# A two-layer decoder trunk on one core: the even mixer's queues woven together, I - X by VectorE and the inverse copied by ScalarE

## The chip, the cores and the metric

The kernel runs on one core of a Trainium2 chip. The metric is the device time of one execution in microseconds (us). TensorE multiplies matrices into PSUM, eight banks of 512 float32 columns; VectorE, ScalarE and GpSimd do elementwise work; SyncE issues the weight transfers. Each engine works through its own queue in order and waits on semaphores.

## The reference

512 tokens of width 1024 pass two layers. Each is: half a gated feed-forward product, a mixer, the other half product, and a gated embedding term; a norm ends it. The mixer of layer 0 (even) joins sliding-window attention and an RWKV-7 recurrence, that of layer 1 (odd) is a forgetting attention. What the change touches is the recurrence, 8 heads of 64:

```python
def step(state, inp):
    r_t, w_t, k_t, v_t, kk_t, a_t = inp
    s_kk = einsum('bhij,bhj->bhi', state, kk_t)
    state = state * w_t - s_kk * (kk_t * a_t) + v_t * k_t
    return state, einsum('bhij,bhj->bhi', state, r_t)
...
y = (y - mean) * rsqrt(var + GN_EPS) * ln_w + ln_b
y = y + sum(r * k * r_k) * v
out = concat([attention, y * g]) @ even_w_out
```

## The kernel before, in words

All float32 weights are used as a sum of two reduced parts: ScalarE writes `w_hi` (`split_hi`), VectorE `w_lo = w_raw - w_hi` (`split_lo`), and a tile of 128 columns costs three matmuls (`product`, L421). Weights come in jobs: SyncE loads a job's tiles into one of two slots, ScalarE and VectorE split it when the job two before is done, TensorE multiplies. In the even mixer's input projection a job has 16 tiles and fills two banks; in the output projections 8 tiles and one.

The even mixer runs in this order. `even_tensor` (L779) computes the projection in 160 groups of three matmuls, and between groups the attention of four head pairs; `even_scalar`, `even_vector` and `even_pool` hold the matching orders as strings (L920, L1048, L1097: J is a job's evictions and split, L logits, E exponentials, M a token-shift mix, S its difference on GpSimd). Then `rwkv_tensor`, `rwkv_scalar`, `rwkv_vector` and `rwkv_pool` (L1152 to L1619) treat the recurrence in chunks of 64 tokens, in two halves `h` of four heads, each as two pairs `q`, one half wholly behind the other (`rwkv_start`, L1147, waits for the half before). Within a half:
- the front: decays and scaled keys (`lora`, `sigmoids`, `lc`, `exps`, `kq`, `b_scaled`, `rq`, `k_scaled`, `rk_summed`, `bonus`) and their transposes (`turned`, L1200), which end in `ab` and `ak`, the products within chunks;
- the inverse of a triangular 64x64 block for each head and chunk, in levels 1 to 5. A level is X = A M (L1264), a mask on X by VectorE, M X' and X' M^T (L1270, L1272), and two subtractions by VectorE that renew `m_inv` and `mt_inv`;
- the output products `we`, `gq`, `h`, `yc`, and a chain of states over the chunks (`z`, L1301, and `state`, L1506), each step waiting for the other engine;
- the tail: `yz`, the gate `g`, the group norm (`y_raw` to `gn_normed`), `y_turned`, `y_weighted`, and the split into `y_hi` and `y_lo`.

The output projection's first two jobs are begun early (`out_begin`, L703), in the second half's tail. A step's semaphore counts all steps of its engine, so `due` (L1118) waits for one count of one engine. The table `RWKV_STEPS` (L73) is that order.

Of the kernel before, what the change touches and what calls it, by code (L numbers as in the profile page):

```python
# [62 lines left out]
def both(names):  # L63

    return [f"{name}:{q}" for name in names.split() for q in range(2)]


def each_pair(names):

    return [f"{name}:{q}" for q in range(2) for name in names.split()]  # L70


RWKV_STEPS = {  # L73
    "tensor": both("lora v_turned ss rk_summed kq_turned b_turned k_turned ab ak aab f")
    + [s for n in range(1, LEVELS - 1) for s in both(f"x{n}") + each_pair(f"mx{n} mxt{n}")]
    + both("x5 mxt5 we gq h yc") + [s for c in range(2, NC) for s in both(f"z{c}")]
    + both("yz g y_turned"),
    "scalar": both("""kk_squared sigmoids decay exps chunk_ends kq_by_token k_by_token f_copied we_copied
        h_copied yc_copied g_copied gn_squared gn_std"""),
    "vector": both("""lc lcm ka k rk v_summed v_by_token kk_clamped rn2 kq b_scaled rq k_scaled bonus  # L80
        b_by_token ab_masked ak_masked init m0""")
    + [s for n in range(1, LEVELS - 1) for s in both(f"x_masked{n}") + each_pair(f"m{n} mt{n}")]
    + both("x_masked5 mt5 gq_copied") + [s for c in range(1, NC) for s in both(f"state{c}")]
    + both("bonus_gated y_raw gn_summed gn_rinv gn_normed y_weighted y_done"),
    "pool": both("a_decayed masks_scaled b_tail k_tail diag mt_masked mt0"),
# [27 lines left out]
def trunk(nc, dram, out, stages=STAGES):  # L113

    ctx = ExitStack()
    with ctx:
# [10 lines left out]
        for st in stages:  # L127
# [104 lines left out]
        hb = view("hb", [P, 3 * RP, T + 1])  # L232
# [6 lines left out]
        swa_k = [view(f"swa_k{g}", [P, T]) for g in range(2)]  # L239
        swa_v = view("swa_v", [P, T])  # L240
        swa_vt = view("swa_vt", [P, NB, P])
        swa_logit = view("swa_logit", [P, 2, NB, 2 * P])
# [10 lines left out]

        constants_at = max(offset[0], int(behind_projections * 1024) + 16 * 1024 + 512)
        offset[0] = constants_at
# [4 lines left out]
        gn_eps = view("gn_eps", [P, 1])  # L260
        at(Y + 8)
# [3 lines left out]

        at(XN)
        kr = view("kr", [P, 2, 2, T])  # L270
        amb = view("amb", [P, 2, NC, 3, C])
        kf = view("kf", [P, 2, NC, 2, C])
        mt_inv = view("mt_inv", [P, 2, NC, C])
        at(W + 4)
        m_inv = view("m_inv", [P, 2, NC, C])
        at(W + 12)
        x1 = view("x1", [P, 2, NC, C])
        at(behind_projections)
        bk = view("bk", [P, 2, 2, T])
        ktok = view("ktok", [P, 2, NC, C])  # L280
        vtok = view("vtok", [P, 2, NC, C])
        chunk_end = view("chunk_end", [P, 2, NC])
        v_sum = view("v_sum", [P, 2, NC])
        rn2 = view("rn2", [P, 2, NC])
        gn_sum = view("gn_sum", [P, 2, NC])
        gn_dev = view("gn_dev", [P, 2, NC])
        gn_inv = view("gn_inv", [P, 2, NC])
        assert offset[0] <= constants_at
        at(Y + 12)
        bonus = view("bonus", [P, 2, T])  # L290
# [761 lines left out]
        def even_pool(pool, st):  # L1052
# [1206 lines left out]
```

## Time and profile before

| | before |
|---|---|
| median of 3 runs (lowest, highest) | 2234.67 us (2231.94, 2236.96) |
| profiled execution, its span | 2235.76 us, 2234.1 us |
| TensorE busy, matmuls | 2147.3 us (96%), 12522 |
| VectorE, ScalarE, GpSimd busy | 1126.0, 746.0, 347.8 us |
| mean granted clock of TensorE | 0.98 |
| even mixer, input projection to output projection | about 380 to 760 us of the span |
| odd mixer's output projection | from about 1764 us |

A row of the profile gives a source line, an engine, the operation as out<-in by the program's names, and durations. Matmul durations overlap, since matmuls are pipelined: the distance of starts tells the rate. A granted clock of 1.00 is 2.4 GHz, 0.50 is 1.2 GHz. "[5.64 <-...]" behind a row of the timeline is the engine's idle time ahead of it and what ended it.

### The profile page before, as it was taken

To read this page: it belongs to the slowest core of one execution; us is meant where nothing else is said; L and a number is where in the kernel's file an instruction comes from. 1 tells how busy PE (TensorE), PEld (TensorE's weight loads), DVE (VectorE), ACT (ScalarE), POOL (GpSimd) and SP (SyncE) were. 2 spreads that over 40 slices of the span, in tenths; PEclk is the share of its full clock that TensorE was granted. 3 is DMA by queue.
4 is the path that set the end of the run, shared out by engine and by line. 5 is a ranking of instruction groups with operands and counts; after the bars stand their busy time and mean duration, and the time that the engine had idled before them with its cause. 6 is when DMAs were issued, how large, how long until landed. Compare 5 with 4: busy or idle time off the path is not lost.

```text
span 2234.1 us, 32237 instructions
## 1 busy us (share of the span) xinstructions
PE 2147.3 (96%) x12522; PEld 1746.5 (78%) x12522; DVE 1126.0 (50%) x1337; ACT 746.0 (33%) x968; POOL 347.8 (16%) x352
## 2 busy tenths in 40 slices
PE   7999999996868999999999999999999899999998
PEld 6888888775857888888887888887667688888887
DVE  4443445556685644344565433445666454424464
ACT  4432223343122333122254422223444343312234
POOL 2000004444130300000330000013333320000032
PEclk9999999997979999999999999999999999999999
DMA  5323324320000433332333334324322143243232
GB/s 152 94 80 109 95 84 113 95 57 20 4 2 12 132 94 82 106 107 79 86 111 91 95 92 113 94 71 109 94 75 66 57 132 101 83 118 94 67 94 85
DMA packets 365116, 192.29 MB, mean 86 GB/s; under 512 B 9694, under 2 KB 362064, under 8 KB 365024
## 3 DMA queue, kind: packets, MB, share of 16 engines
q1 hardware_dynamic: 362784, 185.10, 30.0%
q0 software_dynamic: 2224, 5.86, 0.8%
q8 instruction: 70, 1.15, 0.2%
q14 instruction: 22, 0.18, 0.0%
q10 hardware_dynamic: 16, 0.00, 0.0%
HBM read 188.81 MB, written 2.13 MB: 85 GB/s over the span
## 4 chain that ended last, share of the span: by engine, by line
PE 92%; DVE 5%; ACT 2%; issue 1%; DMA 0%; POOL 0%; SPq 0%; ACTq 0%; POOLq 0%; DVEq 0%
PE bank L427 24%; PE bank L428 24%; PE bank L429 24%; PE bank L1182 3%; PE bank L1683 2%; PE bank L1685 2%; PE bank L1684 2%; PE bank L795 2%; PE bank L797 2%; PE bank L796 2%; PE bank L1700 1%; PE bank L1719 1%; PE bank L1730 1%; DVE w_lo L417 1%; ACT w_hi L412 1%
## 5 line engine op out<-in xcount | busy, mean ns | idle before, releaser
L427 PE MATMUL bank<-xn_hi,w_hi 128*128 128x512 f32 x1416 | 554.9, 392 | 10.9 <-DVE w_lo L2190 6.0
L428 PE MATMUL bank<-xn_hi,w_lo 128*128 128x512 f32 x1416 | 552.6, 390 | 0.0
L429 PE MATMUL bank<-xn_lo,w_hi 128*128 128x512 f32 x1416 | 552.4, 390 | 0.0
L412 ACT CAST w_hi<-w_raw 128x2048 fp32r<-128x2048 f32 (+3 forms) x211 | 336.3, 1594 | 624.0 <-PE bank L429 560.1
L417 DVE TENSOR_TENSOR w_lo<-w_raw,w_hi 128x2048 fp32r<-128x2048 f32 (+3 forms) x209 | 441.6, 2113 | 151.2 <-ACT w_hi L412 149.8
L427 PEld LDWEIGHTS bank<-xn_hi,w_hi 128*128 128x128 f32 x1416 | 266.9, 188 | 69.5 <-DVE w_lo L2190 6.3
L428 PEld LDWEIGHTS bank<-xn_hi,w_lo 128*128 128x128 f32 x1416 | 266.8, 188 | 56.1 <-issue 1.0
L429 PEld LDWEIGHTS bank<-xn_lo,w_hi 128*128 128x128 f32 x1416 | 266.8, 188 | 55.7
L429 PE MATMUL bank<-h_lo,w_hi 128*128 128x512 f32 x704 | 273.9, 389 | 0.0
L427 PE MATMUL bank<-h_hi,w_hi 128*128 128x512 f32 x704 | 273.9, 389 | 0.0
L428 PE MATMUL bank<-h_hi,w_lo 128*128 128x512 f32 x704 | 273.9, 389 | 0.0
L581 DVE TENSOR_TENSOR act_in<-bank,rinv 128x512 f32<-128x512 f32 x88 | 60.8, 691 | 368.5 <-PE bank L429 368.5
L463 POOL TENSOR_TENSOR sq_sum<-x 128x512 f32<-128x512 f32 x8 | 8.3, 1039 | 1325.5 <-DVE x L599 1236.3
L429 PEld LDWEIGHTS bank<-h_lo,w_hi 128*128 128x128 f32 x704 | 132.1, 188 | 27.6
L427 PEld LDWEIGHTS bank<-h_hi,w_hi 128*128 128x128 f32 x704 | 132.1, 188 | 27.4
L428 PEld LDWEIGHTS bank<-h_hi,w_lo 128*128 128x128 f32 x704 | 132.1, 188 | 27.4
L599 DVE SCALAR_TENSOR_TENSOR x<-bank,x 128x512 f32 (+1 forms) x64 | 44.2, 691 | 204.6 <-PE bank L429 204.6
L558 ACT CAST h_hi<-prod 128x512 f32 (+1 forms) x88 | 54.6, 621 | 181.7 <-DVE prod L588 181.7
L427 PE MATMUL bank<-y_hi,w_hi 128*128 128x512 f32 x256 | 102.1, 399 | 7.4 <-DVE w_lo L417 6.0
L429 PE MATMUL bank<-y_lo,w_hi 128*128 128x512 f32 x256 | 100.5, 393 | 0.0
L428 PE MATMUL bank<-y_hi,w_lo 128*128 128x512 f32 x256 | 100.2, 392 | 0.0
L591 DVE TENSOR_TENSOR h_lo<-prod,h_hi 128x512 f32 (+1 forms) x88 | 60.9, 692 | 76.3 <-ACT h_hi L558 76.3
(345 smaller groups left out, 2624.3 us busy)
## 6 DMA issues: line engine op xcount, KB each, us to landing
w_raw<-in_ffn_w_gu_dram SPq DMA_DIRECT2D x176, 512.0 KB, 5.0
w_raw<-in_ffn_w_down_dram SPq DMA_DIRECT2D x64, 384.0 KB, 3.9
w_raw<-in_ffn_w_down_dram SPq DMA_DIRECT2D x64, 320.0 KB, 3.7
w_raw<-in_even_w_in_dram SPq DMA_DIRECT2D x20, 512.0 KB, 4.5
w_raw<-in_ple_w_gate_dram SPq DMA_DIRECT2D x16, 512.0 KB, 3.8
w_raw<-in_fox_w_in_dram SPq DMA_DIRECT2D x16, 512.0 KB, 5.2
w_raw<-in_even_w_out_dram SPq DMA_DIRECT2D x16, 256.0 KB, 3.2
w_raw<-in_fox_w_in_dram SPq DMA_DIRECT2D x16, 256.0 KB, 4.3
```

The costliest lines, as they stand in the source:

```text
L412: nc.scalar.copy(w_hi[slot][:, 0:tiles], w_raw[slot][:, 0:tiles]).then_inc(w_hi_ready, 1)
L417: nc.vector.tensor_tensor(w_lo[slot][:, 0:tiles], w_raw[slot][:, 0:tiles], w_hi[slot][:, 0:tiles].bitcast(F32), ALU.subtract).then_inc(w_r ...
L427: nc.tensor.matmul(dst, w[0], hi[:, k], start=k == 0, stop=False)
L428: nc.tensor.matmul(dst, w[1], hi[:, k], start=False, stop=False)
L429: last = nc.tensor.matmul(dst, w[0], lo[:, k], start=False, stop=k == tiles - 1)
L558: nc.scalar.copy(h_hi[:, ds(j)], prod[:]).then_inc(h_hi_ready, 1)
L581: nc.vector.tensor_tensor(act_in[:], bank[2 * slot][:], rinv[:], ALU.mult).then_inc(act_in_ready, 1)
L591: nc.vector.tensor_tensor(h_lo[:, ds(j)], prod[:], h_hi[:, ds(j)].bitcast(F32), ALU.subtract).then_inc(h_ready, 1)
L795: nc.tensor.matmul(dst, hi, xn_hi[:, k], start=k == 0, stop=False)
L796: nc.tensor.matmul(dst, lo, xn_hi[:, k], start=False, stop=False)
L797: mm = nc.tensor.matmul(dst, hi, xn_lo[:, k], start=False, stop=k == DT - 1)
L1182: mm = nc.tensor.matmul(dst[of_chunk(c), at:at + width], lhsT(j, of_chunk(c)), rhs(j, of_chunk(c)), start=k == 0, stop=k == len(operands) - 1)
```

## The change

1. The even input projection has 20 jobs of 8 tiles and one bank instead of 10 of 16, and the query columns come ahead of the low-rank ones; the recurrence's columns come by halves of heads (keys, receptances, values of the first half first).
2. The recurrence's front is cut into functions, 8 on TensorE, 8 on ScalarE, 11 on VectorE and 4 on GpSimd. The first half's stand between projection jobs (F in the strings), the second half's between the first half's levels. The first half's tail stands between the second half's levels. Tiles of the two halves lie apart, and each group of steps has a semaphore of its own (`RWKV_SEMAPHORES`, `seen`).
3. The levels: GpSimd masks A beforehand (`a_level`), VectorE makes I - X from PSUM (`one_less_x`), TensorE forms the whole new inverse and its transpose, and ScalarE copies both from PSUM (`level_done`). Before, VectorE masked X and subtracted twice.
4. Between the steps of the second half's chain of states stand groups of the output projection.
5. Both mixers' output projections use the lower and the upper half of the weight buffers in turn, so that a job is split two jobs ahead.

```diff
-                jobs.phase(st + "in", [2 * DT] * (2 + 2 * RP))
+                jobs.phase(st + "in", [DT] * (4 + 4 * RP))
...
-        FIRST_WINDOW, APART = 18, 24
+        FIRST_WINDOW, APART = 27, 22
...
+            between += [(g, part, ()) for g, part in zip((118, 122, 127, 131, 139, 145, 152, 158), front)]
...
-            for what in "J0 E0 J1 J2 C0 E1 H0 J3 C1 E2 J4 H1 J5 C2 E3 H2 J6 C3 J7 H3".split():
+            for what in ("J0 J1 T0 J2 J3 J4 E0 J5 J6 C0 J7 E1 T1 H0 J8 J9 C1 E2 J10 H1 J11 F0 J12 C2 E3 J13 H2 F1 F2 "
+                         "J14 F3 J15 F4 C3 F5 J16 H3 F6 J17 J18 F7 J19").split():
...
+            for what in ("J0 J1 J2 L0 J3 J4 D0 J5 L1 J6 J7 T1 D1 V0 J8 L2 J9 M0 J10 M1 V1 D2 L3 J11 M2 J12 M3 V2 "
+                         "J13 M4 D3 M5 F0 J14 F1 F2 J15 F3 M6 F4 V3 J16 F5 M7 F6 F7 F8 J17 M8 F9 J18 M9 F10 "
+                         "J19 M10 M11").split():
...
+            for what in "N0 N1 S0 S1 S2 N2 S3 S4 S5 N3 S6 F0 S7 F1 S8 F2 F3 S9 S10 S11".split():
...
-                    for q in range(2):
-                        due(dve, f"x{level}", h, q)
-                        tt(x1[:, q], by_chunk(rb(q, 2)[:]), mask(MASK_L + level), ALU.mult, f"x_masked{level}")
...
-                            tt(m_inv[:, q], m_inv[:, q], by_chunk(rb(q, 3)[:]), ALU.subtract, f"m{level}")
...
-                        tt(mt_inv[:, q], mt_inv[:, q], by_chunk(rb(q, 0)[:]), ALU.subtract, f"mt{level}")
+            def one_less_x(h, level):
+                for q in range(2):
+                    level_seen(dve, "x", h, level, q)
+                    if level > 1:
+                        level_seen(dve, "mxt", h, level - 1, q)
+                    nc.vector.tensor_tensor(m_x[:, q, 1], over_chunks(eye[:]), by_chunk(rb(q, 2)[:]), ALU.subtract
+                                            ).then_inc(R["x_copied"], 1)
...
+            def level_done(h, level):
...
+                        nc.scalar.copy(m_x[:, q, 0], by_chunk(rb(q, 3)[:])).then_inc(R["m"], 1)
...
+                    nc.scalar.copy(mt_inv[:, q], by_chunk(rb(q, 0)[:])).then_inc(R["mt"], 1)
...
+            def a_level(h, level):
...
+                    nc.gpsimd.tensor_tensor(a_lev[:, q], am0[h][:, q], over_chunks(masks[:, MASK_LT + level]),
+                                            ALU.mult).then_inc(R["a_level"], 1)
...
+        def upper(j):
+
+            return j // 2 % 2
...
+            for n, j, slot, ahead in out_jobs(st):
+                if j + 2 < DT:
+                    out_split_hi(act, st, j + 2)
+                    gain_hi(act, norms[st] + 1, j)
```

TensorE's queue behind the first half's `ab` and `ak`, up to level 2. Before (`x` is the masked X):

```order
L1171 MATMUL bank<-kr,bk 64x128 x64
L1182 MATMUL bank<-eye,amb 64x64 x32
L1182 MATMUL bank<-vtok,akm 64x64 x32
L1182 MATMUL bank<-m_inv,amb 64x64 x32
L1182 MATMUL bank<-x,mt_inv 64x64 x16
L1182 MATMUL bank<-mt_inv,x 64x64 x16
L1182 MATMUL bank<-x,mt_inv 64x64 x16
L1182 MATMUL bank<-mt_inv,x 64x64 x16
L1182 MATMUL bank<-m_inv,amb 64x64 x32
```

Now (`m_x` holds the inverse and I - X; L1212 is `lora_w`, L1219 `lora_a`, L1198 `v_turned`, all of the second half):

```order
L1456 MATMUL bank<-kr,bk 64x128 x64
L1469 MATMUL bank<-eye,am_0 64x64 x32
L1469 MATMUL bank<-vtok,akm 64x64 x32
L1212 MATMUL bank<-th,lora_wa 128x512 x2
L1469 MATMUL bank<-m_x,a_lev 64x64 x32
L1219 MATMUL bank<-th,lora_wa 128x512 x2
L1469 MATMUL bank<-m_x,mt_inv 64x64 x16
L1469 MATMUL bank<-mt_inv,m_x 64x64 x16
L1469 MATMUL bank<-m_x,mt_inv 64x64 x16
L1469 MATMUL bank<-mt_inv,m_x 64x64 x16
L1198 MATMUL bank<-ident,hb 128x128 x8
L1469 MATMUL bank<-m_x,a_lev 64x64 x32
```

The second half's front moved into the first half's levels. VectorE's queue there, levels 1 to 3, now (L1841 is `one_less_x`, the rest the second half's front):

```order
L1841 TENSOR_TENSOR m_x<-eye,bank 128x512 x2
L1322 SCALAR_TENSOR_TENSOR act_in<-chunk_start,kr 128x512
L1322 SCALAR_TENSOR_TENSOR other<-chunk_start,kr 128x512
L1326 TENSOR_TENSOR kr<-act_in,kr 128x512
L1326 TENSOR_TENSOR kr<-other,kr 128x512
L1348 TENSOR_REDUCE v_sum<-bank 128x8 x2
L1352 SCALAR_TENSOR_TENSOR vtok<-v_sum,bank 128x512 x2
L1841 TENSOR_TENSOR m_x<-eye,bank 128x512 x2
L1332 TENSOR_SCALAR bk<-tmp,vecs 128x512 x2
L1336 SCALAR_TENSOR_TENSOR tmp<-bk,hb 128x512 x2
L1359 TENSOR_SCALAR rn_1<-bank 128x8 x2
L1363 RECIPROCAL rn_1<-rn_1 128x8 x2
```

Before, this queue had the masks and the subtractions of the levels and nothing else.

## Rows read from the trace of the kernel before

**Rows 1.** The page: busy time of each engine, share of the span, instructions.

```profile
PE 2147.3 (96%) x12522; PEld 1746.5 (78%) x12522; DVE 1126.0 (50%) x1337; ACT 746.0 (33%) x968; POOL 347.8 (16%) x352
```

**Rows 2.** Stretches of the span: length, busy of each engine, granted clock, DMA share, GB/s.

```profile
519.00:554.00 35.00, 16.34 (x75) 10.03 (x75) 30.12 (x37) 12.16 (x21) 16.36 (x10) 0.66 0.05 15
...
604.00:651.00 47.00, 23.31 (x184) 14.46 (x188) 35.72 (x60) 17.75 (x30) 12.96 (x8) 0.69 0.00 1
...
660.00:703.00 43.00, 40.69 (x1328) 39.35 (x1328) 25.51 (x49) 4.91 (x14) 2.63 (x2) 1.00 0.02 4
...
800.00:820.00 20.00, 20.00 (x90) 16.57 (x89) 9.74 (x10) 8.79 (x8) 0.00 (x0) 1.00 0.28 75
```

**Rows 3.** TensorE's waits, 522 to 722: us in total, times, longest.

```profile
PE bank L1229 <- DVE rn L1440: 17.5, 2, 9.0
```

**Rows 4.** Timeline of TensorE: start, length, line and operation, [idle before <-releaser].

```profile
525.19 1.19 PE L1215 MATMUL bank<-th,lora_wa 64*128 64x512 f32 x1 [5.64 <-issue]
...
544.01 1.04 PE L1202 MATMUL bank<-ident,kr 128*128 128x128 f32 x8
...
553.86 5.42 PE L1171 MATMUL bank<-kr,bk 64*64 64x128 f32 x128
...
563.72 1.15 PE L1182 MATMUL bank<-m_inv,amb 64*64 64x64 f32 x32 [0.70 <-DVE m_inv L1392]
...
590.96 3.60 PE L1182 MATMUL bank<-kf,mt_inv 64*64 64x128 f32 x62
...
603.51 0.40 PE L1301 MATMUL bank<-x,bk 64*64 64x64 f32 x8
...
659.88 1.15 PE L1182 MATMUL bank<-m_inv,amb 64*64 64x64 f32 x32 [0.70 <-DVE m_inv L1392]
...
704.20 1.98 PE L1311 MATMUL bank<-gate_in,lora_g 128*128 128x512 f32 x4
```

**Rows 5.** Timeline of VectorE in the first half's front.

```profile
533.46 0.68 DVE L1397 SCALAR_TENSOR_TENSOR sq<-bk,hb 128x512 f32<-128x512 f32 x1
...
534.66 1.77 DVE L1397 SCALAR_TENSOR_TENSOR bonus<-hb,vecs,sq 128x512 f32<-128x512 f32 x1
...
541.41 2.38 DVE L1397 SCALAR_TENSOR_TENSOR kr<-hb,vecs,tmp 128x512 f32<-128x512 f32 x1
```

**Rows 6.** Timeline of ScalarE in the first half's front.

```profile
526.53 1.28 ACT L1333 ACT_TABLE_LOAD   x1
...
544.64 1.08 ACT L1324 ACTIVATE kf<-bank 128x512 f32<-128x512 f32 x2 [8.94 <-PE bank L1202]
```

**Rows 7.** Timeline of GpSimd ahead of the first half's levels.

```profile
558.60 2.05 POOL L1588 TENSOR_TENSOR kr<-eye,chunk_end 128x512 f32<-128x512 f32 x2 [5.84 <-PE bank L1171]
560.60 2.50 POOL L1588 TENSOR_TENSOR mt_inv<-amb,masks 128x512 f32<-128x512 f32 x2
563.06 3.40 POOL L1588 TENSOR_TENSOR mt_inv<-eye,mt_inv 128x512 f32<-128x512 f32 x2
```

**Rows 8.** Timelines of VectorE and ScalarE at the projection's start and in a job.

```profile
389.02 3.35 DVE L487 RECIPROCAL rinv<-rms 128x512 f32<-128x512 f32 x1 [1.18 <-ACT rms L482]
393.86 2.80 DVE L937 TENSOR_TENSOR swa_k<-bank,rinv 64x512 f32<-64x512 f32 x4 [1.49 <-PE bank L797]
...
506.61 1.21 DVE L417 TENSOR_TENSOR w_lo<-w_raw,w_hi 128x1024 fp32r<-128x1024 f32 x1
...
505.40 1.06 ACT L412 CAST w_hi<-w_raw 128x1024 fp32r<-128x1024 f32 x1 [3.47 <-PE bank L797]
```

**Rows 9.** Timeline of TensorE at both mixers' output job 2.

```profile
722.98 0.49 PE L427 MATMUL bank<-y_hi,w_hi 128*128 128x512 f32 x1 [2.65 <-DVE w_lo L417]
...
1768.58 0.49 PE L427 MATMUL bank<-y_hi,w_hi 128*128 128x512 f32 x1 [3.34 <-DVE w_lo L417]
...
1769.56 0.63 PE L427 MATMUL bank<-y_hi,w_hi 128*128 128x512 f32 x1
```

**Rows 10.** DMA issues: line, count, KB each, median us to landing, 392 to 519.

```profile
w_raw<-in_even_w_out_dram SPq DMA_DIRECT2D x6, 256.0 KB, 3.1
```

More of the change, by code:

```diff
@@ L59 @@
     """.split()
[L63 to L85, printed above, removed]
+RWKV_SEMAPHORES = {
+    "front_products": "lora_w lora_a v_turned ss rk_summed kq_turned b_turned k_turned",
+    "front_activations": "kk_squared sig_w sig_a decay exps chunk_ends kq_by_token k_by_token",
+    "front_decays": "lc lcm", "front_values": "v_summed v_by_token", "front_norms": "kk_clamped rn2",
+    "front_elements": "ka k rk kq b_scaled k_scaled bonus rq b_by_token",
+    "front_tails": "a_decayed b_tail k_tail masks_scaled",
+    "pair_products": "ab ak aab f", "pair_masks": "ab_masked ak_masked init m0", "inverse_start": "mt_masked mt0 diag",
+    "f_copied": "f_copied", "a_level": "a_level", "x": "x", "x_copied": "x_copied", "mx": "mx", "mxt": "mxt",
+    "m": "m", "mt": "mt",
+    "chunk_products": "we gq h yc", "chunk_copies": "we_copied h_copied yc_copied", "gq_copied": "gq_copied",
+    "z": "z", "state": "state",
+    "tail_products": "yz g y_turned", "tail_activations": "gn_squared g_copied gn_std",
+    "tail_elements": "y_raw gn_summed bonus_gated gn_rinv gn_normed y_weighted y_done",
 }
@@ new lines, in rwkv_tensor @@
+            xs(1, 2)
+            yz(0, 1)
+            ms(1, 2)
+            xs(1, 3)
+            g(0)
+            ms(1, 3)
+            xs(1, 4)
+            ms(1, 4)
+            y_turned(0)
+            xs(1, 5)
+            ms(1, 5)
+            w_and_e(1)
+            gq(1)
+            hs(1)
+            yc(1)
+            for c in range(1, NC - 1):
+                z(1, c)
+                if c > 1:
+                    out_begin(pe, st, 0, c - 2, c - 1)
+            out_begin(pe, st, 0, NC - 3, OUT_BEGUN["even"])
@@ new lines, in rwkv_vector @@
+            front[5]()
+            one_less_x(0, 4)
+            front[6]()
+            front[7]()
+            front[8]()
+            one_less_x(0, 5)
+            front[9]()
+            front[10]()
+            gq_copied(0)
+            states(0)
+            ab_masked(1)
+            ak_masked(1)
+            start_inverse(1)
+            one_less_x(1, 1)
+            y_raw(0, 0)
+            one_less_x(1, 2)
+            y_raw(0, 1)
+            gn_summed(0)
+            one_less_x(1, 3)
@@ L1610, in rwkv_pool @@
[L1610 to L1619 removed]
+                    seen(pool, "ab", h, q)
@@ L1625, in unit_cols @@
+            front = rwkv_front_pool(pool, st, 1)
+            start_inverse(0)
+            a_level(0, 1)
+            diag(0)
+            a_level(0, 2)
+            front[0]()
+            a_level(0, 3)
+            a_level(0, 4)
+            front[1]()
+            a_level(0, 5)
+            front[2]()
+            front[3]()
+            start_inverse(1)
+            a_level(1, 1)
+            diag(1)
+            for level in range(2, LEVELS):
+                a_level(1, level)
         def unit_cols(u):
```

1315 lines of the change are left out of this document (796 added, 519 removed).

## The prediction

> **What bounds the kernel now.** I read the page first: TensorE is busy for 2147.3 of 2234.1 us and VectorE for half of it [rows 1]. So a gain can only come from stretches in which TensorE idles or runs slowly. The table by stretches shows two, both in the even mixer [rows 2]: TensorE is busy 16.3 of 35 us from 519 to 554 and 23.3 of 47 us from 604 to 651, with a granted clock of 0.66 and 0.69; in the inverse levels (660 to 703) it is busy 40.7 of 43 us at full clock. The waits name what ends the idle time: 17.5 us in two waits of `rk_summed` (L1229) for VectorE [rows 3]. The timeline [rows 4] tells the order: projection and attention end at 519.6 (the row at 525.19, less its idle 5.64), the first half's own products begin at 553.86, its levels at 563.72, its output products at 590.96, its chain of states at 603.51, and the second half's levels only at 659.88. The weights are not the bound: 256 KB land in 3.1 us [rows 10], one projection job's worth in two such transfers.
>
> **The change, part by part.** I compare the same marks before and after. All is worked out against the profiled execution (2235.8 us, span 2234.1), 1.1 above the median of the runs. "Front" is the elementwise and turning work ahead of `ab`, "half" a set of four heads.
>
> (a) *The first half's front moves under the projection.* TensorE still has to do it: six products 512 wide (1.98 for two, so about 5.7), 32 transposes (8 in 1.04, less at full clock, about 3.5) and `ss` (16 narrow ones, set at 0.8): 10 us [rows 4]. Now it is between projection groups. New waits, from the orders of the queues:
> - Jobs of 8 tiles halve the time in which a bank must be emptied and the next weights split. At the start VectorE ends the reciprocal at 392.4, then needs 2.8 for `swa_k`, which empties job 0's bank, and 1.2 for job 2's `w_lo`: 396.4 [rows 8]. TensorE is through with jobs 0 and 1 (the 16 groups that were one job) at 393.8, where `swa_k` began. Cost 2.6.
> - `v_by_token` stands on VectorE behind the split of job 15, and `ss` waits for it: 2.6. `kq_turned` waits for `bonus`, fourth in a block of five pieces: 1.9. The last bank must be emptied before `ab`: 0.8.
> The other jobs I take as covered: 24 matmuls at 20 us for 90 [rows 2] are 5.4 us, ScalarE's half split is 1.06 and VectorE's 1.21 [rows 8], a pass over a bank 0.68 [rows 5], so 2.4 us are left in each job for what stands ahead in the queue. `ab` begins at 519.6 + 10 + 7.9 = 537.5 instead of 553.9: **gain 16.4**.
>
> (b) *From `ab` to the first level.* Before: 9.9 us. Now VectorE has two tiles left to mix, and GpSimd must make `mt_masked`, `mt0` and the masked copy `a_lev` before the first product; the first two took 2.50 and 3.40 for the two pairs of heads, the cheapest op there half of 2.05 [rows 7]. 1.3 for `ab`, 3 for the mixing and `ab_masked`, 5.9 and 1.2 on GpSimd and the hand-overs give 12.1: **loss 2.2**.
>
> (c) *The first half's levels, with the second half's front inside.* The levels alone took 27.2. The inverse is now copied by ScalarE (half of 1.08 a copy [rows 6]) and I - X made by VectorE (one pass of 0.6 where three stood), both shorter than TensorE's 16 products (27.2 us for 28 such sets, 0.97): the split of the work as such is worth nothing, because the levels were TensorE-bound. It frees VectorE 2.4 us a level, in which the front fits. TensorE gets 8.1 more (10 less the `lora_w` products that fall into b). Waits: `sig_a` is behind the whole first level on ScalarE, and `v_turned` behind it, 1.9; `a_lev` and `bonus` about 1.1. Then VectorE and GpSimd slow each other: the same form of VectorE op takes 0.68 alone and 1.77 and 2.38 while GpSimd works [rows 5, 7]. With 16 such ops in the stretch the bounds are 0 and 16 times 1.4, 22 us. I take 6, nearer the low end, as TensorE has work queued between most of them. 27.2 + 8.1 + 3 + 6 = 44.3: **loss 17.1**.
>
> The Trainium skill (SBUF — State Buffer, on the engine ports) says that VectorE ops with two SBUF inputs and GpSimd ops that read SBUF take one shared port pair in turn, each for its whole length. By that rule VectorE can be held no longer than GpSimd works: 16 ops of this stretch at half of 2.05, 16.4 us instead of my bound of 22, and the sum would be 2207 at worst; the trace agrees in kind, 1.77 for 0.68 beside an op of GpSimd.
>
> (d) *Output products* of each half: as before, 0.4 for a wait on `k_by_token`: **loss 0.4**.
>
> (e) *Between the halves.* From the first chain of states (603.51) to the second half's first level (659.88) there were 56.4 us of tail, front and `ab`. Now the front is done and the tail comes later. What is left: six steps of the chain, with the two `ab` of the other half between them, 6.3; then `ab_masked` (VectorE, four passes of half width, 1.4 a pair of heads by the 0.68 of a whole one), `mt_masked`, `mt0` and `a_lev` on GpSimd, 8.5, with 4 us of TensorE work within. 14.8: **gain 41.6**.
>
> (f) *The second half's levels, with the first half's tail inside.* 27.2 + 4.2 for `yz`, the gate (1.98) and `y_turned`; the fourth I - X stands behind `gn_normed` on VectorE, which waits for a square root behind level 3 and a table load (1.28, [rows 6]) on ScalarE: 4: 35.4, **loss 8.2**. The chain of states takes 5.9 instead of 3.9, since output-projection groups stand between its steps: **loss 2.0** (they come back in g).
>
> (g) *The tail of the second half.* Before, from the last state (703.1, just ahead of the gate product's 704.20) to output job 2 at 722.98: 19.9 us, 2.65 of them for its `w_lo` [rows 9]. Now `y_raw` doesn't wait for the gate, no table load stands in it, 4 us of output groups are done, and job 2's weights go to the buffers' upper halves and are split before job 0's result is wanted. 13.3: **gain 6.6**.
>
> (h) *The odd mixer's output projection* gets the same early split: 3.34 of waiting goes, and the slow matmuls behind it (start to start 0.43 instead of 0.23, some eight of them): **gain 5.0** [rows 9].
>
> Sum: 16.4 - 2.2 - 17.1 - 0.4 + 41.6 - 8.2 - 2.0 + 6.6 + 5.0 = 39.7. 2235.8 - 39.7 = **2196 us**.
>
> **The rivals.**
> - *VectorE and GpSimd as the bound of the first levels.* If the slowing costs 14 instead of 6, and 4 more under the projection, where the first half's front meets the evictions and splits: 2208. For it: 1.77 and 2.38 in rows 5. Against: before, TensorE idled there, so every delay showed. Chance 0.25.
> - *The stalls don't come.* The waits of (a), (c) and (f) are worked; of the 7.9, 9 and 4 us, two thirds may not come if the queues interleave better than I see, 14 less: 2182. Chance 0.18.
> - *The small projection jobs starve TensorE (slower).* Each of some 18 jobs has 2.4 us to spare, and the attention's exponentials and logits (E and L in the strings) stand whole between the splits. If every job came 3 us late, 54 us would be lost, 2196 + 54 = 2250; it decides the sign from 2.2 us a job. Against: VectorE was busy 50% of the whole [rows 1], and there are four such blocks for 20 jobs. Chance 0.04.
> - *The overlap fails because a shared bank or buffer puts the front back in line:* about half of (e) lost, 2217. Chance 0.04.
>
> **How the numbers follow.** The forecast, 2196 with 2188 to 2204, gets 0.49. The range takes in both neighbouring rivals but not their far ends: 2179 to 2213. Faster by over 0.2% (about what a measurement of this kernel can tell from no change, 4.5 us): all but the starving case and a remnant, 0.95; within it 0.01; slower 0.04.
>
> **What would show it.** `ab` of the first half at about 537, the levels 44 us long at full clock instead of 27, the second half's levels some 15 us behind the first chain of states, no wait for `w_lo` ahead of output job 2 in either mixer, and the granted clock near 1 all through. It is wrong if TensorE waits for `w_lo` in the projection again and again, if the first half's levels take over 52 us, or if idle time above 10 us is left between the halves.

## The result, and the profile after

The changed kernel takes 2217.2 us (median of 4 runs, 2216.4 to 2217.8), the kernel before 2234.2 (2231.9 to 2237.0): ratio 0.9923, 95% interval 0.9906 to 0.9940. It is faster, as forecast, but by 17 us where 39.7 were worked out, and 2217.2 lies above the range (2179 to 2213). The profiled execution took 2217.2 (span 2215.6), 18.5 less in span than before.

The page of the changed kernel, busy time of each engine:

```profile
PE 2151.0 (97%) x12778; PEld 1749.5 (79%) x12778; DVE 1106.0 (50%) x1319; ACT 766.2 (35%) x1013; POOL 374.3 (17%) x376
```

Its stretches of the even mixer: from:to, length, busy time (number) of TensorE, its weight load, VectorE, ScalarE and GpSimd, granted clock, DMA share, GB/s.

```profile
392.40:519.60 127.20, 117.81 (x633) 90.48 (x632) 80.04 (x115) 58.23 (x130) 51.65 (x63) 0.97 0.23 67
519.60:548.75 29.15, 23.20 (x101) 17.64 (x99) 19.88 (x23) 6.48 (x9) 16.00 (x11) 0.89 0.12 36
560.40:605.00 44.60, 39.76 (x954) 35.17 (x954) 30.91 (x41) 19.43 (x35) 24.22 (x17) 0.96 0.01 3
605.00:632.40 27.40, 22.43 (x816) 21.05 (x816) 14.07 (x36) 6.39 (x17) 10.76 (x10) 1.00 0.02 4
632.40:671.70 39.30, 34.01 (x972) 32.15 (x972) 15.63 (x25) 13.76 (x24) 14.08 (x11) 0.91 0.01 4
```

The two dead stretches of [rows 2] are gone: from 605 to 632.4, between the halves, TensorE is busy 22.4 of 27.4 us. But the projection, 2.3 us from full before, is not: from 392.4 to `ab` TensorE idles 15.3 of 156.35 us. The timeline of TensorE shows where, and the marks that answer to [rows 4], the moments at which a part begins: start, length, operation, [idle before <-releaser].

```profile
395.67 0.80 PE L831 MATMUL bank<-xn_hi,w_hi 128*128 128x512 f32 x1 [2.77 <-DVE w_lo L410]
...
508.46 1.54 PE L874 MATMUL bank<-ident,swa_p 128*128 128x128 f32 x6 [3.49 <-ACT swa_pt L950]
...
528.70 1.23 PE L1198 MATMUL bank<-ident,kr 128*128 128x128 f32 x8 [1.40 <-DVE bonus L1391]
...
543.46 1.94 PE L1198 MATMUL bank<-ident,tmp 128*128 128x128 f32 x8 [3.77 <-DVE btok L1398]
545.05 0.78 PE L831 MATMUL bank<-xn_hi,w_hi 128*128 128x512 f32 x1
545.62 0.63 PE L832 MATMUL bank<-xn_hi,w_lo 128*128 128x512 f32 x1
...
548.75 0.49 PE L1456 MATMUL bank<-kr,bk 64*64 64x128 f32 x4 [0.79 <-DVE hb L995]
...
560.41 1.15 PE L1469 MATMUL bank<-m_x,a_lev 64*64 64x64 f32 x32
...
595.80 1.23 PE L1198 MATMUL bank<-ident,kr 128*128 128x128 f32 x8 [1.90 <-DVE act_out L1391]
...
604.98 3.89 PE L1469 MATMUL bank<-kf,mt_inv 64*64 64x64 f32 x126 [0.33 <-ACT ktok L1313]
...
619.01 0.22 PE L1587 MATMUL bank<-am,bk 64*64 64x64 f32 x1
...
632.43 1.15 PE L1469 MATMUL bank<-m_x,a_lev 64*64 64x64 f32 x32 [1.96 <-POOL a_lev L2031]
...
661.33 1.58 PE L1469 MATMUL bank<-m_x,mt_inv 64*64 64x64 f32 x32 [4.74 <-DVE m_x L1841]
...
671.72 3.89 PE L1469 MATMUL bank<-kf,mt_inv 64*64 64x64 f32 x126
...
686.27 0.40 PE L1587 MATMUL bank<-am,bk 64*64 64x64 f32 x8
...
693.95 1.16 PE L1456 MATMUL bank<-am,bk 64*64 64x64 f32 x64
...
705.05 0.50 PE L420 MATMUL bank<-y_hi,w_hi 128*128 128x512 f32 x1 [3.04 <-DVE y_lo L1909]
...
709.35 0.53 PE L420 MATMUL bank<-y_hi,w_hi 128*128 128x512 f32 x1
```

`kr` turned is `kq_turned`, the two `tmp` are `b_turned` and `k_turned`. 548.75 is `ab`, 560.41 and 632.43 the first level of each half, 604.98 and 671.72 their output products, 619.01 and 686.27 their chains of states, 709.35 the output projection's job 2, which now waits for no `w_lo`. Why `k_turned` was late stands in the timeline of VectorE:

```profile
537.81 1.46 DVE L410 TENSOR_TENSOR w_lo<-w_raw,w_hi 128x1024 fp32r<-128x1024 f32 x1
541.20 1.51 DVE L1076 SCALAR_TENSOR_TENSOR hb<-act_out,vecs,hb 128x512 f32<-128x512 f32 x1 [1.94 <-POOL act_out L1130]
542.64 1.27 DVE L1398 TENSOR_TENSOR btok<-bank,rn 128x512 f32<-128x512 f32 x2
```

and in that of GpSimd:

```profile
533.80 6.37 POOL L1435 TENSOR_TENSOR am<-masks,rn 128x512 f32<-128x512 f32 x4
540.13 1.03 POOL L1130 TENSOR_TENSOR act_out<-hb 128x512 f32<-128x512 f32 x1
```

VectorE stood from 539.3 to 541.2 in front of a tile to mix, whose shift GpSimd made only behind its four scaled masks; `b_by_token`, for which TensorE waited, was the next piece in VectorE's queue; what it reads had been ready since 535.6, when TensorE ended `b_turned`. The 3.49 at 508.46 is of the same kind: ScalarE copied the first turned probabilities (507.35) behind the four exponentials `exps` (505.26 to 507.4).

The marks give each term of the sum its measured size:

| term | forecast | measured | from |
|---|---|---|---|
| (a) `ab`, first half | +16.4 | +5.1 | 553.86 to 548.75 |
| (b) to the first level | -2.2 | -1.8 | 9.86 to 11.66 |
| (c) first half's levels | -17.1 | -17.3 | 27.24 to 44.57 |
| (d) output products, first half | -0.4 | -1.5 | 12.55 to 14.03 |
| (e) between the halves | +41.6 | +43.0 | 56.37 to 13.42 |
| (f) second half's levels | -8.2 | -12.1 | 27.2 to 39.29 |
| its output products | 0 | -2.5 | 12.05 to 14.55 |
| its chain of states | -2.0 | -3.7 | 3.94 to 7.68 |
| (g) last state to output job 2 | +6.6 | +4.5 | 19.87 to 15.40 |
| (h) odd mixer's output projection | +5.0 | +4.4 | lead 14.1 ahead of it, 18.5 at the end |
| sum | +39.7 | +18.1 | span: 18.5 |

The largest miss is (a), 11.3 of the 21 us. Of the rest, (f) is 3.9, the output products of both halves 3.6, the chain 1.7 and (g) 2.1. In (h), the lead is by how much the changed kernel is ahead at the odd mixer's first output product and at the end.

The marks count from the start of the span, and executions do not reach the mixer at the same moment: TensorE's first projection product starts at 381.80 before and at 380.96 now. Counted from there `ab` comes after 172.1 and 167.8 us, so that 0.8 of the 5.1 in (a) arose ahead of the mixer.

### The profile page after: what moved, and what is told of

It reads as the page before. It is cut to its first block, busy times and chain, and to the rows that moved or that the text cites. A ratio compares the mean times of both kernels' runs of the same rounds, so it can differ in the third digit from the quotient of the medians.

```text
span 2215.6 us, 32685 instructions
## 1 busy us (share of the span) xinstructions
PE 2151.0 (97%) x12778; PEld 1749.5 (79%) x12778; DVE 1106.0 (50%) x1319; ACT 766.2 (35%) x1013; POOL 374.3 (17%) x376
## 3 DMA queue, kind: packets, MB, share of 16 engines
HBM read 188.81 MB, written 2.13 MB: 86 GB/s over the span
## 4 chain that ended last, share of the span: by engine, by line
PE 91%; DVE 3%; ACT 2%; issue 2%; POOL 2%; DMA 0%; SPq 0%; POOLq 0%; DVEq 0%; ACTq 0%
PE bank L420 25%; PE bank L422 24%; PE bank L421 24%; PE bank L1469 3%; PE bank L2113 2%; PE bank L2115 2%; PE bank L2114 2%; PE bank L831 1%; PE bank L2130 1%; PE bank L833 1%; PE bank L832 1%; PE bank L2149 1%; PE bank L2160 1%; DVE w_lo L410 1%; ACT w_hi L405 0%
## 5 line engine op out<-in xcount | busy, mean ns | idle before, releaser
L405 ACT CAST w_hi<-w_raw 128x2048 fp32r<-128x2048 f32 (+3 forms) x209 | 325.7, 1559 | 637.8 <-PE bank L422 560.0
L410 DVE TENSOR_TENSOR w_lo<-w_raw,w_hi 128x2048 fp32r<-128x2048 f32 (+3 forms) x207 | 423.3, 2045 | 148.1 <-ACT w_hi L405 147.2
L420 PEld LDWEIGHTS bank<-h_hi,w_hi 128*128 128x128 f32 x704 | 132.2, 188 | 27.4
L592 DVE SCALAR_TENSOR_TENSOR x<-bank,x 128x512 f32 (+1 forms) x64 | 44.3, 692 | 205.6 <-PE bank L422 205.6
```

The costliest lines, as they stand in the source:

```text
L405: nc.scalar.copy(w_hi[slot][:, 0:tiles], w_raw[slot][:, 0:tiles]).then_inc(w_hi_ready, 1)
L410: nc.vector.tensor_tensor(w_lo[slot][:, 0:tiles], w_raw[slot][:, 0:tiles], w_hi[slot][:, 0:tiles].bitcast(F32), ALU.subtract).then_inc(w_r ...
L420: nc.tensor.matmul(dst, w[0], hi[:, k], start=k == 0, stop=False)
```

## The experiments

Theory Q: what is missing was lost to the order of the queues, an instruction that was ready behind one that was not. Theory E: the engines, slowed by each other, are at their limit, and a wait that is removed comes back elsewhere. The kernel before had medians of 2233.4 to 2234.0 beside these runs.

**The changed kernel again.**

> The changed kernel itself beside the others: 2217, within 1 us of its earlier runs. It measures how far the chips and runs of one kernel differ, under either theory.

Measured: 2217.8 (2215.7 to 2222.3). A difference of 1 us between medians says nothing here; marks in the traces say more. Counted from the first projection product, `ab` comes after 167.3 us here and 167.8 in the first trace. But the first half's levels take 46.1 here and 44.6 there, the same instructions at a granted clock of 0.93 and 0.96:

```profile
560.40:606.50 46.10, 41.25 (x954) 36.61 (x954) 30.90 (x41) 19.44 (x36) 24.26 (x17) 0.93 0.01 3
```

So half a us in the place of `ab` means something, 1.5 us in the length of these levels does not.

**ScalarE's copies of the probabilities first.**

```diff
-"J14 F3 J15 F4 C3 F5 J16 H3 F6 J17 J18 F7 J19"
+"J14 F3 K0 J15 K1 F4 F5 J16 H3 F6 J17 J18 F7 J19"
```

K0 and K1 are the two halves of C3, the copies of the fourth pair.

> ScalarE copies the turned probabilities of the fourth pair before the four exponentials of the decay, and its first two copies before the split of job 15's turn. Theory Q (the missing time under the projection is set by the order of the queues): the wait of 3.49 us ahead of the second set of probability transposes (508.46) goes, and with it the slow clock behind it, about 1 us; `ab` begins 4 us earlier, near 544.5, and the kernel takes 2213. Theory E (the engines, slowed by each other, are the limit): the exponentials are later by the two copies, `a_decayed` and what follows on VectorE are as late as before, the wait comes back at `kq_turned` or `k_turned`, and `ab` stays within 1 us of 548.75.

Measured: 2217.0 (2215.0 to 2218.8), no change. The wait went and another came 1.2 us behind its place (timeline of TensorE):

```profile
509.70 1.47 PE L1233 MATMUL bank<-head_ones,bk 128*128 128x2 f32 x12 [3.04 <-DVE vtok L1352]
```

This is the wait of `ss` for `v_by_token`, which the prediction had priced at 2.6 and the changed kernel did not show: both were there, one behind the other. `ab` came at 547.26, 1.5 earlier (1.1 counted from the first projection product). By this run alone theory E looks right.

**`b_by_token` ahead of the ninth tile.**

```diff
-"... J18 M9 F10 J19 M10 M11"
+"... J18 F10 M9 J19 M10 M11"
```

> VectorE makes `b_by_token` before it mixes the ninth tile, so it no longer stands behind a tile whose shift GpSimd makes only after its 6.4 us of scaled masks. Theory Q: the wait of 3.77 us ahead of `k_turned` (543.46) shrinks to under 1, and the granted clock of 0.50 from 545 to 550 rises; `ab` begins 5 us earlier (3 of wait, 2 of clock), 543.5, kernel 2212. Theory E: the mixing is still as late, the last job's split behind it too, and the gain is under 1.5 us.

Measured: 2210.8 (2209.1 to 2211.6), 7 us off for two pieces exchanged in VectorE's queue. The timeline of TensorE:

```profile
539.61 1.23 PE L1198 MATMUL bank<-ident,tmp 128*128 128x128 f32 x8 [0.33 <-DVE btok L1398]
543.01 1.21 PE L1456 MATMUL bank<-kr,bk 64*64 64x128 f32 x36 [0.78 <-DVE hb L995]
```

3.4 of wait is gone, and `ab` is 5.7 earlier (5.2 if one takes off that this execution had started the mixer 0.56 sooner). The levels behind it took 43.0 instead of 44.6, so that 1.6 of the 7 us may be their spread. Theory Q, and a term that the prediction had not under the projection: the clock.

**Matmuls that compute nothing.** Twelve of them in front of `k_turned`, added to the changed kernel.

```diff
+                if h == 0:
+                    for i in range(12):
+                        nc.tensor.matmul(bank[4][:], xn_hi[:, 0, 0:P], xn_hi[:, 0], start=True, stop=True)
```

> The changed kernel with twelve matmuls of 128x512 that compute nothing (into a free bank) put ahead of TensorE's turning of `k`, where it idled 3.77 us; at 0.23 each they fill 2.7 of them. They add work that the output does not use. If the granted clock of 0.62 from 540 to 550 comes from TensorE's own idle time ahead of it, it stays near 1, `ab` begins 1.5 to 2.5 us earlier than 548.75 and the kernel takes 2215 to 2216. If the clock falls for another reason, `ab` stays within 0.5 us.

Measured: 2213.9 (2211.9 to 2215.9), 3 to 4 us faster than without them; `ab` at 546.24. The timeline of TensorE, the filler and what follows it:

```profile
538.93 2.88 PE L1260 MATMUL bank<-xn_hi 128*128 128x512 f32 x12
542.85 1.23 PE L1198 MATMUL bank<-ident,tmp 128*128 128x128 f32 x8 [1.04 <-DVE btok L1401]
```

The stretch from 540 to 550 with the filler (columns as above):

```profile
540.00:550.00 10.00, 8.14 (x150) 6.49 (x149) 6.83 (x9) 3.46 (x5) 2.59 (x3) 1.00 0.01 2
```

The same stretch of the changed kernel without the filler:

```profile
540.00:550.00 10.00, 5.75 (x38) 4.68 (x42) 4.33 (x5) 3.18 (x5) 3.21 (x4) 0.62 0.00 1
```

The wait ended no sooner (542.85, in an execution that ran 0.55 ahead), but the granted clock stayed at 1 and the work behind it ran at full speed: 0.98 for the eight transposes instead of 1.59, 0.23 a matmul instead of 0.43. So an idle 3.8 us costs 3.8 and then 2 more. The rest of the 3 to 4 us is not in this trace, which is of the slowest of the four executions. The Trainium skill (TensorE: Matmul & The Clock Gate, on the HAM clock gate) says that a gate sets the clock by how busy TensorE has been of late; here the trace agrees.

**GpSimd's scaled masks ahead of its tails.** They got a semaphore of their own for it.

```diff
-"N0 N1 S0 S1 S2 N2 S3 S4 S5 N3 S6 F0 S7 F1 S8 F2 F3 S9 S10 S11"
+"N0 N1 S0 S1 S2 N2 S3 S4 S5 N3 S6 F0 S7 F3 F1 S8 F2 S9 S10 S11"
```

> The changed kernel with one edit on GpSimd: the four scaled masks (6.4 us, from 533.8) are made ahead of the tails of `b` and `k`, in the 15 us in which GpSimd idled before 526. What the wait of `k_turned` (3.77) rests on: under the order theory the ninth tile's shift comes some 4 us earlier, VectorE's two `rq` passes run alone (1.3 for both instead of 2.98), the wait shrinks to under 1, and the kernel takes 2211 to 2213, as with `b_by_token` moved. If the slowing of VectorE by GpSimd is what costs, it moves to the passes that now run beside the masks and the gain is under 3 us: 2215 or more.

Measured: 2210.1 (2207.2 to 2218.2). The wait of `k_turned` is 0.66, `ab` at 542.30, 5.2 earlier counted from the first projection product, as with `b_by_token` moved; the four masks took 4.05 instead of 6.37, in a stretch where VectorE idled, and the two `rq` passes 2.13 instead of 2.98 (1.3 was expected). The same wait goes from the other end of the chain, as theory Q says.

**The last pair's values and the elementwise work early,** on top of `b_by_token` moved.

```diff
-ScalarE: "... J16 H3 F6 ..."     VectorE: "... F4 V3 J16 F5 M7 F6 F7 F8 J17 ..."
+ScalarE: "... H3 J16 F6 ..."     VectorE: "... F4 F5 F6 F7 V3 J16 M7 F8 J17 ..."
```

> On top of `b_by_token` ahead of the ninth tile, ScalarE rounds the last pair's attention output before the split of job 16's turn, and VectorE scales `kq`, `b` and `k` ahead of the low part of that output, in the 6.7 us in which it idled before 521. Theory Q (queue order): the wait of 1.40 for `bonus` ahead of `kq_turned` goes, GpSimd's tails and scaled masks start up to 8 us earlier, no wait is left at `k_turned`; `ab` begins 1.5 to 2 us before its 543.0 of the run with `b_by_token` moved alone, and the kernel takes 2209 against 2210.8. Theory E (engine limit): the ops that were moved run beside GpSimd now and lose what they gain; 2210.8 stays.

Measured: 2210.7 (2207.9 to 2215.5). No wait is left at `kq_turned` or `k_turned` and `ab` comes at 541.37, 1.6 before the 543.01 and 2.4 counted from the first projection product; the medians can't show it. Worked by the trace, a small yes for theory Q.

**The fourth I - X of the second half first.**

```diff
             bonus_gated(0)
-            gn_normed(0)
             one_less_x(1, 4)
+            gn_normed(0)
```

> In the second half VectorE makes the fourth I - X before it normalises the first half's tail. Theory Q: the wait of 4.74 us at 661.33 goes and the slow clock behind it (1.5 us) too; a new wait of up to 1.5 us stands at the tail's transposes; the second half's levels take 34 to 36 us instead of 39.3 and the kernel 2212. Theory E: GpSimd's last level mask and VectorE's gate product (3.36 us for two) hold the level anyway, and the levels stay above 38.

Measured: 2214.8 (2213.8 to 2215.5), 3 us off instead of 6; the levels take 38.0, where the two traces of the changed kernel have 39.3 and 38.8, so the trace shows only about 1 of the 3. The wait shrank from 4.74 to 3.29 only, because `bonus_gated`, the gate product, still stood ahead (timeline of VectorE):

```profile
658.04 3.36 DVE L1876 SCALAR_TENSOR_TENSOR bonus<-bonus,vecs,tail_g 128x512 f32<-128x512 f32 x2 [5.16 <-ACT tail_g L1733]
661.32 1.27 DVE L1841 TENSOR_TENSOR m_x<-eye,bank 128x512 f32<-128x512 f32 x2
```

VectorE idled 5.16 for ScalarE's copy of the gate, and the two passes took 3.36 beside GpSimd's level mask, 1.40 for the same two in the second half's tail, where GpSimd rested.

**All orders at once.** The copies first; `v_by_token` ahead of `rk` and of the split (`F1 F3 J15 F2`); `b_by_token` and the elementwise work as above; the fourth I - X ahead of both `bonus_gated` and `gn_normed`.

> All the moves together: ScalarE's copies of the fourth pair's probabilities ahead of the exponentials, `v_by_token` on VectorE ahead of the split of job 15's turn (it took the place of that wait when the copies alone were moved: 3.04 us), `b_by_token` ahead of the ninth tile, the early elementwise work, and in the second half's levels the fourth I - X ahead of both the gate product and the normalisation. Theory Q: waits of 3.5, 3.8 and 1.4 under the projection and of 4.7 in the levels are gone, each with its slow clock; `ab` begins at 538 to 540 (the predicted 537.5), the second half's levels take 34 to 35, and the kernel takes 2202 to 2205. Theory E: the waits come back elsewhere, 2208 or more.

Measured: 2199.6 (2196.2 to 2203.4), 18 us less than the changed kernel and 2.4 below what was expected; ratio to before 0.9845 (0.9827 to 0.9864). TensorE's waits from 392 to 549: us in total, times, longest.

```profile
PE bank L831 <- DVE w_lo L410: 3.3, 2, 2.8
PE bank L857 <- DVE swa_logit L1029: 2.4, 2, 1.7
PE bank L1469 <- DVE am L1807: 1.3, 2, 1.1
PE bank L1456 <- DVE hb L995: 0.8, 1, 0.8
PE bank L1198 <- DVE bonus L1391: 0.6, 1, 0.6
```

The stretches of the same run: projection, first and second half's levels.

```profile
392.40:536.80 144.40, 137.17 (x732) 105.19 (x732) 100.96 (x137) 64.65 (x138) 68.70 (x74) 0.99 0.23 66
548.40:594.50 46.10, 41.28 (x952) 36.63 (x952) 30.90 (x41) 19.36 (x36) 24.28 (x17) 0.93 0.01 3
622.00:655.00 33.00, 32.47 (x972) 30.52 (x972) 14.54 (x25) 13.60 (x24) 13.58 (x11) 0.95 0.02 4
```

`ab` begins at 536.8, 156.4 us behind the first projection product where it was 167.8, and the second half's levels take 33.0 with nothing for TensorE to wait for. The engines had room for this front; the order did not use it. Theory E falls here. The copies moved alone had gained nothing only because the next instruction in line was late too.

**The value tile first,** on top of that.

```diff
-            firsts = [SWA_Q, SWA_Q + P] + ...
+            firsts = [SWA_Q + P, SWA_Q] + ...
```

> On top of all the moved orders, the projection turns out the attention's value tile first and its key tile second, so that the first bank is emptied by one pass of VectorE behind the reciprocal instead of four (0.7 instead of 2.8). If the first wait (2.77 us at 395.7) is set by that emptying and the split behind it, it shrinks to 0.5 to 1 and the second job's four passes are hidden behind job 2's 5.4 us of matmuls: 2 us earlier, 2197.5. If job 3 then waits for the same passes, nothing is gained: 2199.6.

Measured: 2196.2 (2195.5 to 2201.2), ratio to before 0.9836 (0.9813 to 0.9859): the fastest that was found, with the next one. The projection's first wait is 0.79 instead of 2.77, one of 0.15 came at 412, and `ab` begins at 532.4, 3.5 earlier counted from the first projection product, where 2 were expected: the wait that went is 2.0, and the slow clock behind it 1.5. The stretch from 390 to 400 of the changed kernel:

```profile
390.00:400.00 10.00, 7.23 (x25) 5.57 (x24) 7.43 (x8) 1.04 (x1) 8.61 (x22) 0.83 0.36 107
```

and of this run:

```profile
390.00:400.00 10.00, 9.21 (x43) 7.29 (x42) 6.98 (x10) 2.69 (x3) 8.62 (x21) 1.00 0.38 107
```

**The turned tiles behind the levels' products,** on top of the value tile first.

```diff
-            front[2]()
             xs(0, 2)
+            front[2]()
             ms(0, 2)
```

and `kq_turned` behind `xs(0, 5)`, `b_turned` behind `ms(0, 5)`, VectorE's `one_less_x(0, 2)` ahead of `front[3]`.

> On top of the kernel with the value tile first, in the first half's levels TensorE turns `v` behind the second level's first product and `kq` behind the fifth's, instead of ahead of them. The waits of 1.37 for `sig_a` and 1.90 for `bonus` go, since TensorE has the level's products before them; if the slow clock that follows them (0.83 in some 10 us) is their doing, 1.5 us more: 4 to 5 us off, 2193 to 2194. If the levels' own products then wait for VectorE's copies instead, because the turned tile no longer fills the gap, under 1 us is gained.

Measured: 2195.6 (2195.2 to 2200.5): nothing gained. The 1.37 and 1.90 are gone and so much came in their place, in three waits of TensorE for GpSimd's level mask; the levels took 46.9 instead of 46.0. TensorE's waits from 545 to 593:

```profile
PE bank L1469 <- POOL a_lev L2031: 4.5, 3, 2.3
```

0.5 of the 4.5 was there before. This trace is of the slowest of the four executions, 2200.5. The second expectation held in its size, but the wait is for GpSimd and not for copies: the turned tile had hidden GpSimd's 2.5 us, and here GpSimd is the next in line.

**Output weights late again,** one part of the change undone: each output job's weights are loaded to the lower half of the buffer and split behind the result of the job two ahead.

```diff
-                if j + 2 < DT:
-                    out_split_hi(act, st, j + 2)
                 gain_hi(act, norms[st] + 1, j)
+                act.wait_ge(job_done, n + 1)
+                split_hi(act, n + 2, slot, ahead)
```

> The changed kernel with one part undone: both output projections load and split the weights of a job only behind the result of the job two ahead, in the lower half of the buffer, as before. Predicted from the terms (g) and (h): the even mixer's output job 2 waits again 2.65 for its split (and up to 1.5 of slow clock), the odd mixer's 3.34 and the slow matmuls behind it, 4.4 measured between the two traces; in all 7 to 8.5 slower than 2217.8: 2225 to 2226. If the even mixer's tail had been set by something else, only the odd mixer's 4.4 would come back: 2222.

Measured: 2226.2 (2221.5 to 2227.8), 8 us slower. The profiled execution was the fastest of the six, 2221.5; in it the odd mixer lost 3.04 at output job 2 and the slow matmuls behind, but the even mixer only 1.17 (timeline of TensorE):

```profile
708.45 0.50 PE L420 MATMUL bank<-y_hi,w_hi 128*128 128x512 f32 x1 [1.17 <-DVE w_lo L410]
```

The size is as forecast, but the trace of this one execution has only some 5 us of it; where the others lost more stays open.

**VectorE makes the copies, second half.**

```diff
+                if h in BY_VECTOR:      # (1,)
+                    for q in range(2):
+                        if level + 1 < LEVELS:
+                            level_seen(dve, "mx", h, level, q)
+                            nc.vector.tensor_copy(m_x[:, q, 0], by_chunk(rb(q, 3)[:])).then_inc(R["m"], 1)
+                        level_seen(dve, "mxt", h, level, q)
...
+                        nc.vector.tensor_copy(mt_inv[:, q], by_chunk(rb(q, 0)[:])).then_inc(R["mt"], 1)
```

> In the second half's levels alone VectorE, not ScalarE, copies the new inverse and its transpose from PSUM. Predicted: the split of the work as such is worth nothing where VectorE has time, as a set of copies is shorter than TensorE's 16 products; the second half's levels stay within 1.5 us of 39.3 and the kernel within 1.5 of 2217.8. The rival (the split pays by itself, because copies and I - X no longer stand in one queue): each level waits about one copy, 0.7, for the other: 3 to 6 us slower.

Measured: 2219.1 (2218.2 to 2222.2), 1.2 slower; the levels take 40.5, 1.2 more, of which 1.64 is a wait for `y_weighted` behind them.

**VectorE makes the copies, first half.** The same with `(0,)`.

> The first half's levels, with the second half's front inside, and VectorE instead of ScalarE copies the new inverse and its transpose there: 18 more passes of 0.6 to 0.69 us, 11 to 12 us, on an engine that was busy 31 of these 45 us. Predicted (the split is worth nothing by itself but makes the room in which the front fits): the front's pieces come later, the waits at `v_turned`, `kq_turned` and the copies of the inverse grow, the levels take 50 to 54 instead of 44.6 and the kernel 2223 to 2227. Rival (VectorE has room enough for both): within 2 us of 2217.8, as in the second half, where the same edit cost 1.2.

Measured: 2237.7 (2235.4 to 2239.7), 20 us slower than the changed kernel and by 0.16% (0.07 to 0.26) slower than before: this alone gives the whole gain back. The levels took 63.9 us. Their stretch:

```profile
559.80:623.60 63.80, 44.85 (x952) 40.26 (x952) 40.38 (x59) 9.33 (x17) 22.36 (x17) 0.87 0.01 2
```

VectorE is busy 40 of 64 us, so it is not full, as TensorE is not. Neither expectation fits.

**The same, the front's piece ahead of the copies.**

```diff
             one_less_x(0, 2)
             front[1]()
+            level_copied(0, 2)
             front[4]()
```

and so in each level: one piece of the front (two in the fourth) between I - X and the copies.

> As in the run that cost 20 us, VectorE copies the new inverse and its transpose in the first half's levels, but each level's first piece of the front stands ahead of the copies in its queue, where VectorE idled for TensorE's products, instead of behind them. If the 20 us were the order (the front stood behind copies that waited for TensorE), most comes back: first half's levels 50 to 53 instead of 63.9, kernel 2224 to 2227. If they were the load (18 passes of 0.69, 12.4 us, on an engine already busy 31 of 45), little does: levels over 58, kernel 2232 or more.

Measured: 2224.1 (2222.6 to 2224.8), 6 to 7 us slower than the changed kernel. The stretch of its levels:

```profile
559.70:609.70 50.00, 40.69 (x954) 35.97 (x955) 41.47 (x59) 9.40 (x18) 24.24 (x17) 0.93 0.01 3
```

VectorE did the same 59 instructions in 50 us instead of 64. So 14 of the 20 us were order: copies that waited for TensorE's products with the front behind them, and the slow clock after the waits (0.87 against 0.93; TensorE's busy time is 4.2 shorter). What the copies cost on VectorE where they stand well is 3.9 to 5.4: 50.0 for the 46.1 and 44.6 of the changed kernel's two traces, of which the first is at the same clock of 0.93.

## Why the prediction was wrong, point by point

**(a) is the step that failed:** "`ab` begins at 519.6 + 10 + 7.9 = 537.5". It began at 548.75, 29.15 behind 519.6. TensorE idled 15.3 us on the way instead of 2.3 in the kernel before, 13.0 more where 7.9 were counted. Three of the four waits named were right or nearly (2.77 for 2.6, 1.40 for 1.9, 0.79 for 0.8); the fourth, `v_by_token`, was hidden behind one not seen. Two of 3.49 and 3.77 were missed: ScalarE's copies behind the exponentials, and `b_by_token` behind a tile to mix behind GpSimd's masks. The sentence that let them through is "The other jobs I take as covered": it set an average of 2.4 us to spare a job against pieces one by one, and not the block of them that stands ahead in the queue. The rest is busy time, 141.0 against 124.9, 16.1 more where 10 were counted: the front's own products and transposes 10.6 by their starts (`ss`, "set at 0.8", took 1.71), and the slow clock behind three waits about 4.9: 2.0 by the run with the filler, 1.4 between 508.46 and 512.04, and 1.5 behind the first wait by the run with the value tile first. The kernel before had one such stretch of its own, 0.83 from 460 to 470, an estimated 1.5, so that some 2 are not assigned. The prediction priced no clock here, though it did in (h). With the orders mended `ab` came at 536.8, 156.4 us behind the first projection product, where the 537.5 asked for 155.7: it was what the work allows, not what this order gives.

**(b)** held, 11.7 for 12.1. **(c)** held in its sum, 44.6 (46.1 in the second trace) for 44.3, but not in its parts. TensorE waited 4.7 us in it, where 3 for waits and 6 for the slowing of VectorE by GpSimd were added to 0.5; its busy time grew by 13.2 instead of 8.1. The front's pieces took 10.2 by their starts, a product of the fifth level at the slow clock (596.96 to 600.52) 1.7 more than at the full one. So the slowing, real on VectorE (the first two `k` passes 3.44 for 1.28), cost little on TensorE. The worst case by the shared port took 1.0 us (half of 2.05) as the longest that a pass is held; [rows 5] already had a pass held 1.7 (2.38 for 0.68), so that bound was too low, though nothing in the sum hangs on it. "The split of the work as such is worth nothing" was wrong by 3.9 to 5.4 us in the first half, right to 1.2 in the second; "it frees VectorE 2.4 us a level, in which the front fits" is what makes these, and up to 20 in a poor order.

**(d), output products and chain:** 1.1 and 2.5 more than forecast. The second half's idle in its output products is 2.5 us in three gaps that the profile puts down to nothing ("issue", 0.19, 1.46 and 0.82). In the chain each output group takes 0.8 to 0.9 and hides only the 0.2 for which TensorE waited at a step, so 3.7 was lost instead of 2.0, and (g) gained 4.5 instead of 6.6: its last waits, 3.04 for `y_lo`, are a chain of VectorE and ScalarE that no group was left to cover.

**(e)** was the largest term and held: 13.4 for 14.8.

**(f)** The wait named, fourth I - X behind `gn_normed`, came as 4.74 for 4. Not priced was what followed it, 0.83 of granted clock, and the same at 630 to 640. With the orders mended this half takes 33.0.

**(h)** 4.4 for 5.0.

**The rivals.** The time is 2217, the figure given for "a shared bank or buffer puts the front back in line", but not by that cause: (e) came whole. "VectorE and GpSimd as the bound" priced 4 us under the projection, and one part of it is in the trace: the two `rq` passes take 2.98 beside GpSimd's masks and 1.29 in the second half's front, where GpSimd rests. But it was the order that let this reach TensorE. "The small jobs starve TensorE" did not come: from 392 to `ab` two waits for `w_lo`, 3.3 us in all. The waits worked out came, most of them near their size (2.77 for 2.6, 1.40 for 1.9, 4.74 for 4; in (c) 1.37 for 1.9, and 2.4 for 1.1); the list under the projection was short by two, and the rival in which waits are missing from the list was not among the cases, while its opposite, "the stalls don't come", had 0.18.

Of what the prediction said would show it wrong, none came: no repeated wait for `w_lo`, no levels over 52, no 10 us between the halves. These tests looked at the places that had been thought of. Of the signs that it was right, two failed: `ab` at about 537, which points at (a), and a granted clock near 1 all through (0.62 from 540 to 550, 0.96 in the first half's levels).

## What to carry to other kernels

When independent work is woven into a full engine's stream, price the queues, not the engines' spare time: for each piece that the full engine waits for, write out what stands ahead of it in its producer's queue and what *that* waits for, through to the third engine. A wait that is removed and gains nothing may have another one right behind it, so move the whole line of late pieces before the theory is dropped. Compare marks from a point that both traces share, and learn from a second trace of the same kernel which lengths repeat. And count an idle gap of a few us on TensorE with the slow clock that follows it; here it made 3.8 us of waiting into nearly 6.

## What the runs showed of the hardware

With twelve matmuls that compute nothing the kernel was 3 to 4 us faster; 2 of them are seen ahead of `ab`, where the granted clock stayed at 1 over a wait. A shorter wait was followed by a slow clock too: 2.77 us of idle time ahead of 395.67, then matmuls 0.43 apart. In the first half's levels, with the same instructions, the kernel with `b_by_token` moved took 43.0 us at a granted clock of 1.00 and the one with all orders moved 46.1 at 0.93; where such a slow piece falls (550 to 560, 570 to 590, 590 to 600) differed between kernels, with no edit near them, and between two executions of one kernel (44.6 us at 0.96, 46.1 at 0.93). The mean clocks of the runs go with their times: the kernel with the masks early took 2207.2 us at 0.993 and 2218.2 at 0.989, and the 0.004 of the span are 8.8 of the 11 us. What makes the clock differ was not tried.

VectorE passes with two inputs in SBUF took up to 2.7 times as long beside GpSimd: 3.44 for 1.28 (`k`, two), 2.98 for 1.29 (`rq`, two), 3.36 for 1.40 (gate product, two). GpSimd is slowed as well: its four scaled masks took 6.37 beside VectorE's passes and 4.05 where VectorE idled. A pass that reads PSUM did not: in the run with the masks early the two of `bonus` took 1.28 at 526.41, in the middle of GpSimd's 3.69 us at the tails of `b`. The timeline of GpSimd in that run:

```profile
524.71 3.69 POOL L1417 TENSOR_TENSOR tmp<-bk,chunk_end 128x512 f32<-128x512 f32 x2 [4.92 <-DVE bk L1374]
```

and of VectorE:

```profile
526.41 1.28 DVE L1391 TENSOR_TENSOR bonus<-bank,hb 128x512 f32<-128x512 f32 x2
```

The Trainium skill (SBUF — State Buffer, on who interferes with whom) says that a VectorE instruction with at most one SBUF input, outside the two-port modes, does not contend with GpSimd. By that rule the I - X, which reads X from PSUM, is safe from GpSimd; the trace agrees (0.68 to 0.69 for one, in every level). VectorE's copies from PSUM, in the runs in which it made them, took 0.69 each too.

All kernels with the new output products show two or three idle gaps of 0.2 to 1.6 us in those of each half, at nearly the same places, for which the profile names no releaser; the kernel before had 0.8 and 0.3. What they are was not tried.
